# Eight of twelve fixed expert loads issued among the last weights of the first block

## What is computed

```python
def first_block(x, ...):
    h = rms_norm(x, norm1_g[l])
    proj = h @ w_in[l]
    ...
    y_a = o_a @ w_proj_a[l]
    y_b = chunked_gmlp(u, v, ...) @ w_proj_b[l]
    merged = jax.nn.sigmoid(ga) * y_a + jax.nn.sigmoid(gb) * y_b
    x = x + merged @ w_out[l]
    h2 = rms_norm(x, norm2_g[l]).reshape(B * T, D)
    y = hier_moe(h2, ..., w_gate[l], w_up[l], w_down[l])
    return rms_norm(x + y, final_norm_g)

def hier_moe(h, ...):
    ...
    for e in range(N_EXPERTS):
        he = jax.nn.silu(h @ w_gate[e]) * (h @ w_up[e])
        y = y + comb[:, e:e + 1] * (he @ w_down[e])
```

## Time and profile before

| | us |
|---|---|
| median of 3 runs | 1071.7 (1070.44 to 1073.74) |
| the profiled execution | 1075.82 |
| its span in the trace | 1074.1 |
| TensorE busy | 991.3 (92%) |
| VectorE, ScalarE, GpSimd busy | 413.6, 269.5, 177.6 |
| moved by DMA | 226.82 MB, mean 211 GB/s |
| mean granted TensorE clock | 0.958 of full |

### The profile page before, as it was taken

One profiled execution on the slowest core, in us unless ns is written; L12 is line 12 of the kernel. 1 busy time (PEld: TensorE's weight loads), 2 busy tenths in 40 slices (PEclk: granted clock), 3 DMA queues, 4 the chain that ended last, 5 costly groups with the idle time before them and its releaser, 6 DMA issues.

```text
span 1074.1 us, 14527 instructions
## 1 busy us (share of the span) xinstructions
PE 991.3 (92%) x5637; PEld 785.2 (73%) x5637; DVE 413.6 (39%) x928; ACT 269.5 (25%) x630; POOL 177.6 (17%) x159
## 2 busy tenths in 40 slices
PE   4979999999899989766799999999999999999997
PEld 4867877788775645443388887888788888788876
DVE  2149762137732212101452461634315246163422
ACT  2122222201311211111228144123002814412301
POOL 5486997700100000000200000000000000000011
PEclk9888999989989999889899999999999999999999
DMA  7883965638989999999834444322343444432211
GB/s 220 257 259 110 262 219 186 206 116 261 421 348 421 420 421 421 420 421 420 298 113 135 149 154 157 99 98 79 118 149 126 140 143 151 156 109 87 87 51 39
DMA packets 138595, 226.82 MB, mean 211 GB/s; under 512 B 6345, under 2 KB 124450, under 8 KB 126234
## 3 DMA queue, kind: packets, MB, share of 16 engines
q1 hardware_dynamic: 136632, 221.15, 57.6%
q0 software_dynamic: 1600, 4.35, 1.7%
q10 hardware_dynamic: 290, 0.34, 0.1%
HBM read 224.76 MB, written 1.06 MB: 210 GB/s over the span
## 4 chain that ended last, share of the span: by engine, by line
PE 79%; SPq 8%; DVE 5%; DMA 4%; ACT 3%; issue 2%; DVEq 0%; ACTq 0%
PE bank L462 27%; PE bank L1068 10%; SPq L1105 7%; PE bank L931 5%; PE bank L907 5%; PE bank L773 4%; PE bank L679 3%; DMA s<-in_w_up 3%; PE bank L946 3%; PE bank L749 2%; PE bank L809 2%; PE bank L788 2%; DMA ring<-in_w_in 1%; PE bank L572 1%; PE bank L961 1%
## 5 line engine op out<-in xcount | busy, mean ns | idle before, releaser
L462 PE MATMUL bank<-hT,ring 128*128 128x256 f32 x1232 | 277.3, 384 | 0.0
L462 PEld LDWEIGHTS bank<-hT,ring 128*128 128x128 f32 x1232 | 233.6, 192 | 38.1 <-issue 7.1
L1068 PE MATMUL bank<-ring,s 128*128 128x256 f32 x512 | 113.0, 383 | 3.3 <-DVE s L1999 3.3
L1068 PEld LDWEIGHTS bank<-ring,s 128*128 128x128 f32 x512 | 98.3, 192 | 17.3 <-DVE s L1999 3.8
L2150 POOL DMA_DIRECT2D s<-in_final_g x1 | 0.6, 594 | 487.8 <-DVE s L1995 487.8
L773 PE MATMUL bank<-s,z 128*32 128x256 f32 (+1 forms) x448 | 64.1, 430 | 8.2 <-DMA s<-in_w_up 4.5
L1782 DVE SCALAR_TENSOR_TENSOR z<-z,bank 128x256 f32<-128x256 f32 x10 | 4.2, 422 | 162.3 <-ACT z L1309 162.2
L2099 POOL TENSOR_TENSOR ring<-ring,csil 128x2048 f32<-128x2048 f32 x17 | 61.3, 3604 | 18.1 <-PE bank L488 17.2
L931 PE MATMUL bank<-ring,hT 128*128 128x256 f32 x256 | 56.1, 380 | 0.0
L907 PE MATMUL bank<-hT,ring 128*128 128x256 f32 x256 | 55.6, 379 | 0.0
L931 PEld LDWEIGHTS bank<-ring,hT 128*128 128x128 f32 x256 | 48.5, 190 | 7.4 <-issue 0.9
(11 more groups left out here) (408 smaller groups left out, 1508.1 us busy)
## 6 DMA issues: line engine op xcount, KB each, us to landing
ring<-in_w_in SPq DMA_DIRECT2D x56, 1024.0 KB, 5.1
ring<-in_w_ada SPq DMA_DIRECT2D x24, 1024.0 KB, 6.0
ring<-in_w_out SPq DMA_DIRECT2D x20, 1024.0 KB, 5.0
s<-in_w_down SPq DMA_DIRECT2D x18, 1024.0 KB, 21.6
s<-in_w_gate SPq DMA_DIRECT2D x15, 1024.0 KB, 25.3
s<-in_w_up SPq DMA_DIRECT2D x13, 1024.0 KB, 24.3
ring<-in_w_up SPq DMA_DIRECT2D x12, 1024.0 KB, 22.2
ring<-in_w_gate SPq DMA_DIRECT2D x10, 1024.0 KB, 24.6
```

Source lines behind the costliest of these rows:

```text
L462: mm = pe.matmul(b[:, 0:T], w[:, (k0 + kb) * CW + m * P:(k0 + kb) * CW + (m + 1) * P], rhs[:, kb, :], start=(kb == 0), stop=(kb == nk - 1))
L1068: mm = pe.matmul(xo[j, tt][:, 0:CW], yT[:, kb, tt * P:(tt + 1) * P], w[:, kb, :], start=(kh == 0 and kb == 0), stop=(kh == 1 and kb == KB ...
```

## The change

A table says behind which chunks expert loads are issued, and how many: key 10 is chunk 39 (three loads), key 8 is chunk 41 (three), key 3 is chunk 46 (two). The body of the loop over the expert loads becomes a function, `load_expert`, which keeps the waits of `overlaid`; the loop over the chunks calls it, and the later loop skips the eight loads that are done. The remaining four fixed loads and the 84 others stay where they were, and so do all slots, semaphores and waits.

```diff
+EARLY_LOADS = {10: 3, 8: 3, 3: 2}
...
-            for n, parts in enumerate(chunks):
-                load(n, parts)
-                if n == 1:
-                    load_layer_rows()
...
-            ids = {}
-            for n, (j, c) in enumerate(expert_order):
+            ids, early = {}, []
+
+            def load_expert(n):
+
+                j, c = expert_order[n]
                 if n < NM:
                     for sem_value in overlaid.get(slot[E0 + n], ()):
                         sp.wait_ge(*sem_value)
+                load(E0 + n, [expert_part(ids.get(j, j), c)])
+
+            for n, parts in enumerate(chunks):
+                load(n, parts)
+                for _ in range(EARLY_LOADS.get(NB1 - n, 0)):
+                    load_expert(len(early))
+                    early.append(n)
+                if n == 1:
+                    load_layer_rows()
+
+            for n, (j, c) in enumerate(expert_order):
+                if n < len(early):
+                    continue
                 if j >= FIXED and j not in ids:
                     if not ids:
                         sp.wait_ge(B.free, B.upto("order"))
                     ids[j] = sp.value_load(order[0:1, j:j + 1], min_val=0, max_val=EXPERTS - 1)
-                load(E0 + n, [expert_part(ids.get(j, j), c)])
+                load_expert(n)
```

## The result

| | before | changed |
|---|---|---|
| median of 7 runs, us | 1073.74 (1070.44 to 1075.14) | 1078.39 (1075.31 to 1082.03) |
| ratio, with 95% interval | | 1.0052 (1.0028 to 1.0076) |
| profiled execution, span, us | 1074.1 | 1076.3 |
| TensorE's waits for w_out, us | none | 3.17 and 2.01 |
| fourth output step, first 16 matmuls, us | 3.70 at full clock | 6.54, all but its end at half clock |

The kernel got slower by 0.5%, by the ratio 5.6 us (3.0 to 8.2); the two medians are 4.65 apart. The forecast was 3.1, at the lower edge of this interval, and it had given the larger chance, 0.49 against 0.46, to a change of less than 0.3% in either direction.

The account below looks back on a forecast made before the run. The prediction took the expert stage to be bound by transfers, starting when its first routed load is issued. Late weights of 4.1 us less 1.0 coming back gave 3.1: 1071.7 + 3.1 = 1074.8 us (+0.29%), range 1069.8 to 1079.2.

Parts of the forecast that it names:

- what the stage is bound by: Expert stage: bound by its transfers, 420 GB/s at a DMA share of 1.01; 84 routed loads take 209.7 us.
- the change has nothing to gain: Ahead of the routed loads: moving fixed loads forward only moves idle transfer time behind them, by itself gaining nothing.
- The third rival: Start of routed loads: without profiling they queue 1.6 us behind fixed ones, which the change clears; 1070.1 us, chance 0.05.
- where the waits fall: Output projection: TensorE waits 1.7 us for the second w_out and 2.4 us for the fourth.
- the cold clock: Output steps: waits drop TensorE to half clock, 2.8 us more, 1077.6 us; chance 0.17, put at nothing in the sum.
- About 1.0 us comes back.: Behind the fourth output step: with the adds apart, the last square runs 3.0 us later against weights 4.1 late.
- its own border: Whole kernel: about 0.3% (3.2 us) is what a measurement can tell from no change.
- Second w_out (43): Second output step: weights land at 262.5, wanted at 260.81, so TensorE waits 1.7 us.
- the upper bound: Fourth w_out: ring loads at 3.2 us and expert loads at 2.59 land it at 284.7, 6.1 late, 5.1 net.
- Fourth w_out (48): Fourth output step: weights land at 282.7, wanted at 278.63, 4.1 us late in all, the 1.7 included.
- The second rival: Output projection: the weights are in time, the wait shrinking to VectorE's slack of 1 us; 1071.7 to 1073, chance 0.25.
- The rate by size: Load queue: by size alone a backlog of many megabytes would run near 425 GB/s and the weights be in time.

Follow-up runs that it names:

- no_middle: Changed kernel without the three early loads behind chunk 41 (3, 0, 2); no waits, chunk 39's issue to first routed load 71.83 us, ratio to before 1.0009.
- two_two_one: Changed kernel with five early loads, 2, 2 and 1 behind chunks 39, 41 and 46; no waits, ratio to before 1.0003.
- warm_turn: Changed kernel with added matmuls ahead of the second and fourth steps' waits and one transposition moved ahead of router matmuls; one run, 1077.09 us.
- again: The changed kernel measured and profiled once more, nothing altered; waits 2.70 and 0.76 us, ratio to before 1.0062.
- after_warm: Changed kernel with 6 and 4 added matmuls ahead of the second and fourth output steps' waits; waits 1.36 and 0.15 us, ratio to before 1.0055.
- six_two: Changed kernel with its eight early loads placed six behind chunk 39 and two behind chunk 46; wait 5.70 us, ratio to before 1.0069.
- warmgap: Kernel before with 20 added matmuls of 128 columns while TensorE waits for the router's choice; no w_out waits, ratio to before 0.9997.

## Why the prediction was wrong, and what in it was right

*Right: what the stage is bound by, and that the change has nothing to gain.* no_middle and two_two_one moved five loads forward at D = 71.83 and 71.82. The third rival, a backlog of fixed loads before the routed ones, did not come up in any run: every kernel with early loads is as fast as before or slower.

*Right: where the waits fall.* At the second and at the fourth w_out, from a transfer queue served in the order of issue. Without the last two early loads the second wait went, without the middle three both.

What failed is the sum behind these waits. It had D grow by 3.1 us, 4.1 of waits less 1.0 that comes back. In the profiled execution D grew by 8.3, and three steps make the difference.

*Failed: the cold clock was put at nothing in the sum, and as a rival at a chance of 0.17.* "The waits ... are below both, so it probably holds." This is the largest term, 2.8 us. In the six profiled executions with such waits and no added matmuls in them there were eight waits, from 0.76 to 5.70 us, and behind seven of them the clock was down for part of the step, at a cost of 1.5 to 3.1 us each; only over the first wait of the changed kernel, 3.17 us, it held. The one stretch of 2.6 us in the earlier trace rows had been taken as a rule. The Trainium skill (TensorE: Matmul & The Clock Gate, HAM oscillation) describes groups of matmuls that start cold after each wait for a transfer. Seven of the eight waits here agree with it, though its example has longer ones than most of these.

*Failed: "About 1.0 us comes back."* Nothing did. The step looked at VectorE's and ScalarE's work and took TensorE's part of it as ready; TensorE's transposition stands behind 0.8 us of router matmuls in its own order, and the copies wait for it. 0.3 us came back when this was changed (warm_turn). Without this step the forecast of the text would have been 4.1, +0.38%, and on the right side of its own border.

*Mis-sized: the landings.* "Second w_out (43): 262.5; wanted 260.81" and "Fourth w_out (48): ... 282.7": 1.7 and 4.1 us late. The waits measured 3.2 and 5.2 in the changed kernel, 1.1 more in all. Both rates used were good (348 and 418 GB/s in mixed queues); what was missing is that the last of a load's 16 signals falls further behind the first in a full queue. The 2.59 us apiece of the upper bound had such a growth in it already: by first signals the twelve fixed loads come 27.3 / 11 = 2.48 us apart. The upper bound, 284.7, would have held the fourth w_out: 53.74 is 284.0 on the clock of `before`.

*The terms together.* 3.1 + 2.8 (clock) + 1.0 (nothing back) + 1.1 (landings) make 8.0; the 0.3 left is in how the steps' ends lie: in `before` the second and the fourth step each start 0.14 us ahead of the end that the trace gives the instruction before them, and now they start behind a wait. The other profile of the same kernel, `again`, has 6.8: 3.46 of waits, 3.1 of clock and the same 0.3. The measured times, 5.6 (3.0 to 8.2) and 6.7 us (4.1 to 9.3), are of this size, though 8.3 lies just outside the first. They cannot tell the terms apart.

*The rate by size.* The second rival did not come true, nor did what the prediction had drawn beside it from the rates by size of the Trainium skill (DMA: Bandwidth & Descriptors, the section Bandwidth), a backlog near 425 GB/s throughout. In the mixed queue w_out and ada loads stayed at 348 GB/s, close to the 341 that the page has for a transfer of this size, expert loads of the same size ran at 418, and the weights were later than counted, not earlier.

## What to carry to other kernels

Before moving a load forward, ask what the first load that cannot move waits for: where that is a result and not the queue, early loads gain nothing, and each one takes its 2.5 us out of the slack of whatever is queued behind it. Count that slack for every later load in the queue, with 1.5 to 3 us for the last of its signals, and count a wait of TensorE nearly twice, as these traces do, because of the clock. When part of a delay seems to come back behind its stage, follow the order of every engine on the way, that of the engine which was late included.

## What the runs showed of the hardware

- Of the 16 signals of a 1.05 MB load the last came 1.5 to 3.1 us behind the first for w_out and ada loads in a full queue (1.73 for the second w_out of the changed kernel, 2.86 in after_warm), and 0.4 to 0.9 for most loads of `before` up to 287 us. In that time 0.6 MB and more of later loads are moved (11.55 MB at the first signal, 12.15 at the last).
- A lag once there stayed as long as the queue was full: 1.59 to 1.62 us for six loads running in `before`, 0.45 for the loads ahead of them.
- SyncE's issue of a load took 0.37 us in `before` with little in the queue, and up to 10.53 (six_two's first w_out), 7.93 and 6.46 us behind several loads that were not done.
- The clock fell at a wait of 0.76 us and held over one of 3.17, in two executions of the same kernel. In warmgap it stood at 0.51 in a stretch with no idle time, with matmuls of 128 columns behind ones of 36 and of one. With seven matmuls of 256 columns in the same gap of 4.5 us it held, in two executions.
